# General projection units of a two-block transformer kernel as pairs of 64-row passes

## The reference

```python
def swiglu(h, w_gu, w_down):
    gu = h @ w_gu                      # 1024 -> 2 * 2816
    g, u = gu[..., :D_FF], gu[..., D_FF:]
    return (jax.nn.silu(g) * u) @ w_down

# first block: dilated attention, SwiGLU, forgetting attention, SwiGLU
# second block: a gated linear recurrence, then retention
u = h @ w_in          # recurrence: 1024 -> 2 * 1536, and retention: 1024 -> 6144
return y @ w_out      # 1536 -> 1024 and 2048 -> 1024
```

## Time and profile before

| | |
|---|---|
| median of 3 runs | 2230.83 us (2230.78 to 2235.3) |
| the profiled execution, its own time | 2231.59 us |
| its span, first to last instruction | 2229.8 us |
| TensorE busy | 2198.2 us (99%), 10590 matmuls |
| weight loads busy | 1781.1 us (80%) |
| VectorE, ScalarE, GpSimd busy | 1193.1, 830.0 and 463.0 us |
| HBM read | 197.54 MB, 90 GB/s |
| mean granted TensorE clock | 0.997 of full |

### The profile page before, as it was taken

The page is one execution under the profiler, slowest core; times in us unless marked ns, Lnnn a source line. Parts: engine busy times, 40 slices in busy tenths (PEclk is TensorE's granted clock), DMA queues, the critical chain, the costliest instruction groups (busy, mean ns, idle before and its releaser), DMA issues.

```text
span 2229.8 us, 26805 instructions
## 1 busy us (share of the span) xinstructions
PE 2198.2 (99%) x10590; PEld 1781.1 (80%) x10590; DVE 1193.1 (54%) x2045; ACT 830.0 (37%) x1410; POOL 463.0 (21%) x320
## 2 busy tenths in 40 slices
PE   8999999999999999999999999999999999999998
PEld 7788887887888888877777888888787777877877
DVE  4665557666644443355557444433888765443343
ACT  4334333435332222233443232222468363333322
POOL 2542333241401011123334110112202101110100
PEclk9999999999999999999999999999999999999999
DMA  4222224221333333332322333333333322322322
GB/s 154 89 68 77 82 80 119 81 74 52 94 98 101 95 95 99 100 105 77 95 67 81 99 95 95 101 98 95 94 96 96 93 90 76 100 73 79 95 76 85
DMA packets 87899, 201.46 MB, mean 90 GB/s; under 512 B 7736, under 2 KB 46904, under 8 KB 87776
## 3 DMA queue, kind: packets, MB, share of 16 engines
q1 hardware_dynamic: 83184, 189.62, 27.9%
q10 hardware_dynamic: 4592, 10.13, 1.5%
HBM read 197.54 MB, written 2.18 MB: 90 GB/s over the span
## 4 chain that ended last, share of the span: by engine, by line
PE 91%; DVE 4%; ACT 2%; issue 1%; POOL 1%; DMA 1%; SPq 0%; DVEq 0%; ACTq 0%; POOLq 0%
PE PS L580 50%; PE PS L626 6%; PE PS L628 6%; PE PS L627 6%; PE PS L651 2%; PE PS L652 2%; PE PS L653 2%; PE PS L1174 2%; PE PS L722 1%; PE PS L708 1%; PE PS L698 1%; DVE WL L1892 1%; PE PS L967 1%; PE PS L946 1%; PE PS L956 1%
## 5 line engine op out<-in xcount | busy, mean ns | idle before, releaser
L1892 DVE TENSOR_TENSOR WL<-WR,WH 128x1024 fp32r<-128x1024 f32 x353 | 469.0, 1335 | 727.9 <-ACT WH L1222 727.4
L1222 ACT ACTIVATE WH<-WR 128x1024 fp32r<-128x1024 f32 x353 | 369.5, 1056 | 651.5 <-DMA WR<-in_ws 635.3
L580 PE MATMUL PS<-XH,WH 128*128 128x512 f32 x1024 | 401.3, 392 | 0.8 <-DVE RB L2330 0.8
L580 PE MATMUL PS<-XH,WL 128*128 128x512 f32 x1024 | 398.5, 389 | 0.0
L580 PE MATMUL PS<-XL,WH 128*128 128x512 f32 x1024 | 398.4, 389 | 0.0
L580 PEld LDWEIGHTS PS<-XH,WH 128*128 128x128 f32 x1024 | 192.2, 188 | 42.2 <-issue 1.4
L580 PEld LDWEIGHTS PS<-XL,WH 128*128 128x128 f32 x1024 | 192.2, 188 | 41.2 <-issue 1.4
L626 PE MATMUL PS<-XH,WH 128*128 128x512 f32 x544 | 222.4, 409 | 1.8 <-DVE XL L2119 1.1
L580 PEld LDWEIGHTS PS<-XH,WL 128*128 128x128 f32 x1024 | 192.2, 188 | 39.7
L628 PE MATMUL PS<-XH,WL 128*128 128x512 f32 x544 | 214.1, 394 | 0.0
L627 PE MATMUL PS<-XL,WH 128*128 128x512 f32 x544 | 213.3, 392 | 0.0
(11 more groups left out here) (364 smaller groups left out, 3780.7 us busy)
## 6 DMA issues: line engine op xcount, KB each, us to landing
WR<-in_ws SPq DMA_DIRECT2D x281, 512.0 KB, 3.6
WR<-in_ws SPq DMA_DIRECT2D x144, 256.0 KB, 3.2
B_CB<-gates ACTq DMA_DIRECT2D x8, 512.0 KB, 4.1
A_WB<-weight_rows_out ACTq DMA_DIRECT2D x24, 128.0 KB, 3.5
XTOK<-in_x SPq DMA_DIRECT2D x4, 512.0 KB, 6.3
out<-OUT SPq DMA_DIRECT2D x8, 256.0 KB, 2.0
R_D<-in_decay ACTq DMA_DIRECT2D x4, 256.0 KB, 2.6
GAIN<-in_post ACTq DMA_DIRECT2D x1, 512.0 KB, 4.3
```

The source lines that it names most:

```text
L580: mm = pe.matmul(PS[:, bank + o, :], l, r, start=first and kk == 0 and i == 0, stop=last and kk == 1 and i == 2)
L1222: nc.scalar.activation(WH[:, s, :], WR[:, s, :], ACT.Copy).then_inc(hi_ready, 1)
L1892: tt(WL[:, s, :], WR[:, s, :], WH[:, s, :].bitcast(F32), ALU.subtract).then_inc(lo_ready, 1)
```

## The change

`unit` issues its work in another form. The four banks are gone through in four steps `n` with a pair of banks each: (0, 2), (1, 3), (2, 0), (3, 1). In a step the upper half of the array (partitions 0 to 63) adds into the bank `top` and the lower half (partitions 64 to 127) into the bank `low`, in alternate passes of 64 rows, for both `kk` and the three products: 12 passes a step, 48 a unit, each with its own weight load of 64 rows. After steps 2 and 3 every bank has had the sum over both halves. Since a bank is handed from one half to the other, the passes of a step must be finished before the step that takes its banks: a new semaphore `rows_done` and `unit_used` give the waits. `ready(k)` is now asked for in step 0 alone and `free` ahead of steps 0 and 1.

```diff
+        rows_done = sem("rows_done")
...
+            UPPER, LOWER = slice(0, HD), slice(HD, P)
+            split_units = [0]
...
-                for kk in range(2):
-                    k = 2 * kpair + kk
-                    if ready is not None:
-                        ready(k)
-                    for o in range(4):
-                        if free is not None and first and kk == 0:
-                            free(o)
...
-                        for i, (l, r) in enumerate(pairs):
-                            mm = pe.matmul(PS[:, bank + o, :], l, r, start=first and kk == 0 and i == 0,
-                                           stop=last and kk == 1 and i == 2)
-                mm.then_inc(unit_used, 1)
+                for n, (top, low) in enumerate(((0, 2), (1, 3), (2, 0), (3, 1))):
+                    if free is not None and first and n < 2:
+                        free(top)
+                        free(low)
+                    if n == 1 and t:
+                        pe.wait_ge(unit_used, u)
+                    elif n != 1 and 3 * t + (n + 1) // 2:
+                        pe.wait_ge(rows_done, 3 * t + (n + 1) // 2)
+                    for kk in range(2):
+                        k = 2 * kpair + kk
+                        if ready is not None and n == 0:
+                            ready(k)
+                        for i in range(3):
+                            for rows, o in ((UPPER, top), (LOWER, low)):
+                                if stationary:
+                                    l = (WH, WH, WL)[i][rows, s, kk * T + o * P:kk * T + (o + 1) * P]
+                                    r = (hi, lo, hi)[i][rows, k, :]
+                                else:
+                                    l = (hi, hi, lo)[i][rows, k, o * P:(o + 1) * P]
+                                    r = (WH, WL, WH)[i][rows, s, kk * T:(kk + 1) * T]
+                                mm = pe.matmul(PS[:, bank + o, :], l, r, start=first and n < 2 and kk == 0 and i == 0,
+                                               stop=last and n >= 2 and kk == 1 and i == 2)
+                    mm.then_inc(unit_used if n == 3 else rows_done, 1)
```

More of the change, by code:

```diff
@@ L559, in _ @@
         def _(pe):
+            UPPER, LOWER = slice(0, HD), slice(HD, P)
+            split_units = [0]
             def unit(u, kpair, hi, lo, bank, first, last, stationary, ready=None, free=None):
-                s = u % RING
+                s, t = u % RING, split_units[0]
+                split_units[0] += 1
                 pe.wait_ge(lo_ready, u + 1)
-                for kk in range(2):
-                    k = 2 * kpair + kk
-                    if ready is not None:
-                        ready(k)
-                    for o in range(4):
-                        if free is not None and first and kk == 0:
-                            free(o)
[L571 to L578, removed]
-                        for i, (l, r) in enumerate(pairs):
-                            mm = pe.matmul(PS[:, bank + o, :], l, r, start=first and kk == 0 and i == 0,
-                                           stop=last and kk == 1 and i == 2)
```

## The result

| | before | after |
|---|---|---|
| median | 2230.97 us | 2238.86 us |
| runs | 8 (2230.72 to 2235.3) | 8 (2236.15 to 2240.44) |
| profiled execution, its span | 2229.8 us | 2237.5 us |
| TensorE busy, matmuls | 2198.2 us, 10590 | 2205.1 us, 15846 |

What follows compares the result with a forecast made beforehand. TensorE, busy 99% of the span, was taken as the bound, through its matmul pitch. Pitch 0, changeovers 7.6 and earlier bank waits 2.5 us gave +10 us, 2241 us; the 8-in-10 range was 2174 to 2290 us.

Steps and rivals of the forecast that it cites:

- The pitch of a pair: Line 580's matmuls as upper and lower passes: a pair keeps the whole pass's 226.7 ns, 0 us.
- B: Rival for line 580's pairs: the 13.4 ns vanish, pair at 215.7 ns, 2183 us; chance 0.33.
- C: Rival for line 580's pairs: two loads interfere more or pairs cost 3 ns extra, 2257 to 2290 us; chance 0.21.
- D: Rival for line 580's pairs: two fp32r passes don't run side by side, +1192 us, 3433 us; chance 0.12.
- The changeovers: Edges of line 580's 19 stretches, between whole array and halves: 38 added at 0.20 us, 7.6 us.
- The waits for finished passes: Each step's wait for step `n - 2` in `unit`: met about 1 us early, 0 us.
- `free` and `ready` earlier: Earlier demand for banks and slices: 1.4 us lost in the recurrence, 1.1 in retention, `ready` 0; +2.5 us.
- The SwiGLU's wait for bank 3: SwiGLU group: bank 3 wanted 1.36 us in instead of 2.04, after a similar read; 0 us.
- The sum: Whole kernel: 0 + 7.6 + 2.5 = +10 us against the profiled execution, 2241 us.

Runs made afterwards that it cites:

- e3: The changed kernel with all passes of the lower half left out, so half of each sum is missing; 2364.67 us, one run.
- e6: The kernel before, with a stationary operand of 64 columns in place of 128 in both SwiGLU layers' products; 2242.88 us, one run.
- e7: The kernel before, with the stationary weights of `unit` taken as every second column of 256 in place of 128 neighbours; 2256.79 us, one run.
- e2: The changed kernel with every odd unit in the old form of 24 whole passes; 2282.14 us, one run.
- e8: The changed kernel where each step waits for the step right ahead of it, not the one before that; 2563.66 us, one run.
- e1: The changed kernel with bank pairs in the order (0, 1), (2, 3), (1, 0), (3, 2); 2238.62 us, ratio 1.0029 to the kernel before.
- e5: The kernel before, with 384 in place of 512 streamed columns in both SwiGLU layers' products; 2078.87 us, one run.
- e11: The kernel before, with 256 in place of 512 streamed columns in both SwiGLU layers' products; 1975.38 us, one run.

## Why the prediction was right, point by point

**The pitch of a pair.** Forecast 226.7 ns, unchanged; measured 226.4 ns over eleven pairs. Of the rivals, B (215.7 ns), C (229.7 ns and more) and D (one after the other) fall on this number alone. It was the large choice, with B given almost the same chance (0.34 against 0.33). The rows did not settle it, so that it came out this way was in part luck. The reason given for it holds in part. Right was that each half keeps the whole addition, since it has its own stream and its own load (e3: a lone half pass has it). Weaker was the reason behind it, that the load under the stream takes the time in proportion. e6 goes against that, and e7 too, whose loads were no longer. What is shown is a fixed 13.4 ns for every fp32r pass at the full clock and none at half of it, and that a strided load raises it; what makes it stays open.

**The changeovers.** 38 edges of 0.20 us, 7.6 us: the term that decided. Measured 0.20 us in the timeline after, 0.21 on the mean of the nine retention stretches, and 0.25 us with what follows in e2, between fp32r passes on both sides. The other ten stretches cost some 0.2 us each on the mean, by the starts of the passes around them. In one place the reason shows: before, TensorE waited 0.43 us for GpSimd ahead of the sums of squares at 1578.03 us, and after it doesn't, so that much of the loss ahead of it was waited for anyway.

**The waits for finished passes.** Forecast 0, as cover of 1.36 us lay over them; measured 0, and 0.37 us for each step when e8 took the cover away (0.27 was my estimate).

**`free` and `ready` earlier.** +2.5 us in the sum (1.4 in the recurrence, 1.1 in retention). e1 shows by its timeline that this term was right in both places: without the two waits it gains 1.4 and 1.0 us. The SwiGLU's wait for bank 3, counted as 0, does cost something in one of its groups. The timeline after has it between the sixth and the seventh pair:

```profile
602.88 0.40 PE L589 MATMUL PS<-XH,WL 64*128 64x512 f32 x2
603.34 0.50 PE L589 MATMUL PS<-XH,WH 64*128 64x512 f32 x2
```

0.46 us instead of 0.23, and 0.34 to the next start at 603.68: 0.35 us in all. In the other SwiGLU layer the sixth and the seventh pair are at 1220.85 and 1221.09 us, and nothing is lost.

**The sum.** +10 us was forecast; the medians lie 7.9 us apart and the profiled executions 7.7, or some 8.4 at equal clock. Of these, 2.4 us are the two `free` waits, 0.35 bank 3, 3.75 the nine retention stretches, and some 2 us the other ten, where 4.0 had been counted. So the term that came out too high is the changeovers of the first ten stretches; the other 0.7 us between forecast and measurement is the clock.

## What to carry to other kernels

Split a matmul into halves of the array only if there are no 128 rows to sum over: in fp32r a pair costs what a whole pass costs (226.7 ns for 512 columns), and each change between whole and half passes costs 0.2 us. When a pitch has a remainder above its stream, find out first what the remainder belongs to: one run of lone half passes (e3), or one with fewer columns (e5), would have told ahead of the whole change that it can't be hidden. Before a miss of 1 or 2 us is explained by a wait, line up the starts of the same passes in both timelines and look at the granted clock between them: here a dip of 1.6 us made a real gain of 2.4 us look like none.

## What the runs showed of the hardware that was not expected

- Passes on different halves of the array don't start in program order. With three upper passes ahead of three lower ones in the program, the first lower one starts 10 ns behind the first upper one and the total is that of the changed kernel (2240.4 against 2238.86 us); with six ahead of six, the reach at a start was three passes.
- fp32r passes have a fixed 13.4 ns on top of their stream at 512, 384 and 256 columns (226.7, 173.5 and 120 ns) at the full clock, and nothing on top at half of it (427 ns for 512 columns in e3, 213.3 for 256 in e11); full float32 had 2.4 ns.
- In the one run with the lower half of the array unused in half the work (e3), the granted clock fell to 0.82 on the mean in the last third of the kernel, from about 1.00, and the kernel lost 125 us by it. TensorE was busy 770.53 of 784.9 us there. In the 1000 us before, with the same half passes, it was 1.00. That the unused half is the reason is not shown.
- After about 2.3 us of idle time at 1750 us the granted clock drops in some kernels' profiles (0.83 over ten us before and in e1) and not in others (1.00 in the changed kernel). It is worth about 1.6 us between profiles.
